# Early mixing of a feed-forward's partial sums, and three inner layer norms as two VectorE instructions per block

## The chip, the core and the metric

The kernel runs on one core of a Trainium2 chip, and its metric is the device time of one execution, in microseconds. Five engines run their own instruction streams and wait for each other through semaphores: TensorE (PE in the rows), VectorE (DVE), ScalarE (ACT), GpSimd (POOL) and SyncE (SP), which issues most of the weight loads.

## What is computed

One encoder layer on x of 512 tokens by 1024 channels, all in float32: four sublayers, each followed by a layer norm over the channels.

```
x = layer_norm(ALPHA * x + 0.5 * swiglu(x, ffn1...), ln1_g, ln1_b)
x = layer_norm(ALPHA * x + hybrid_mixer(x, ...), ln2_g, ln2_b)
x = layer_norm(ALPHA * x + memory_cross_attention(x, mem, ...), ln3_g, ln3_b)
x = layer_norm(ALPHA * x + 0.5 * swiglu(x, ffn2...), ln4_g, ln4_b)
layer_norm(x, g, b) = (x - mean) * rsqrt(var + 1e-5) * g + b
```

The hidden width of each feed-forward is 2816, that is 22 chunks of 128.

## The kernel before

**Split products.** Every matmul operand is split into a high part (ScalarE copies it to a reduced float32 form) and a low part (VectorE subtracts the high part from the original), and each product is three matmuls: lines 829 to 831. Weights come as "units" of 128x1024: SyncE loads a unit into `raw` (three or four slots; a load waits until the unit that was in its slot has been split), ScalarE's `prep` writes `ring_hi`, VectorE's `split` writes `ring_lo`, TensorE uses the pair. `U_MK` + m are the eight units of the memory's key projection, `U_F`, `U_KS`, ... those of the mixer behind it, `U_MV` + k those of the memory's value projection.

**The down projection of a feed-forward** is done in five groups of four hidden chunks ("quads") by a scheme of seven block products in place of eight. `part_high` and `part_low` split its seven left operands, GpSimd's `differences` makes four combinations of the weight blocks (`t_1`, `t_2`, and two in place in `wd`), `products` multiplies, and `add_products` (line 1940) adds each product's two 128x512 tiles out of the accumulators in PSUM onto its place: a quarter of the residual x, or one of four blocks of `partial`. Product q of the last group sits at position q. After the last group the partial blocks are mixed into the four quarters of x: four sums on GpSimd (`mix_products`, lines 682 to 689) and four on VectorE (`mix`, line 1947). The two hidden chunks that are left over (chunks 20 and 21) go through `hidden`, `end_hi`, `end_lo` and `last_down` (first feed-forward) or, by halves of the tokens, through `closing` (second). `last_down` goes over the four accumulator banks 4 to 7 twice; its second pass waits for `add_down` (line 1858) to take the first pass's tiles out.

**A layer norm** goes by four blocks of 128 tokens. VectorE adds the last tiles, takes `bn_stats` and `bn_aggr` (`block_stats`, lines 1864 and 1866); GpSimd makes 1/deviation and a shift with four 128x1 instructions (`inverse_deviation`, lines 705 to 710); ScalarE's `standardize` (line 1420) writes (x - mean) / deviation; VectorE's `gain` (line 1875) multiplies by `ln_g`; GpSimd's `add_bias` (line 717) adds `ln_b` for three of the four blocks and VectorE (line 1882) for the last. Then TensorE turns the block (line 849), and ScalarE and VectorE split the turned block into `xT_hi` and `xT_lo` (`turned_pair`), the operand of what follows.

The first norm runs beside the key projection: `project(U_MK + m)` for m = 0 to 7, with the turn of block b after unit `AFTER_MK[b]`. The second and third run inside `project_tiles` beside the last tiles of the mixer's and the cross attention's output projection; the fourth is the end of `closing`. All orders are written out by hand: an engine does its list in order, and a wait at one instruction holds everything behind it.

Of the kernel before, what the change touches and what calls it, by code (L numbers as in the profile page):

```python
# [29 lines left out]
D = 1024  # L30
# [31 lines left out]
QUADS = 5  # L62
# [27 lines left out]
POOL_BLOCKS = (TB - 1, TB - 1, TB - 1, 2)  # L90
AFTER_MK = (1, 3, 4, 5)
# [27 lines left out]
LAST_PRODUCTS = ((2, 3, 4, 5, 6, 7, 8), (2, 3, 4, 5, 6, 9, 12))  # L119
LAST_GATE = (9, 7)  # L120
# [11 lines left out]
def product_unit(f, d, q):  # L132
    return quad_unit(f, d, (LOOP_PRODUCTS if d < QUADS - 1 else LAST_PRODUCTS[f])[q])

# [89 lines left out]
def program(nc, t, out, x_spill):  # L224
    ctx = ExitStack()
    with ctx:
# [164 lines left out]
        acc_zero, acc_mixed, tiles_mixed = sem("acc_zero"), sem("acc_mixed"), sem("tiles_mixed")  # L391
# [4 lines left out]
        shift_done = sem("shift_done")  # L396
# [111 lines left out]
        def product_of(n):  # L508

            for f in range(2):  # L510
                for d in range(QUADS):
                    for q in range(PRODUCTS):
                        if product_unit(f, d, q) == n:
                            return f, d, q
            return None
# [133 lines left out]
        def _(pool):  # L649
# [13 lines left out]
            def differences(f):  # L663

                with pool.Fori(0, QUADS) as i:
                    made = 4 * QUADS * f
                    b11, b21, b22, b12 = down_part(0), down_part(1), down_part(2), down_part(5)
                    pool.wait_ge(wd_in[0], upto(16 * QUADS * f + 16, i, 16))
                    nc.gpsimd.tensor_tensor(t_1[:, :, :], b12, b11, ALU.subtract).then_inc(t_made, 1)  # L669
                    pool.wait_ge(wd_in[1], upto(16 * QUADS * f + 16, i, 16))  # L670
# [3 lines left out]
                    pool.wait_ge(unit_lo, upto(product_unit(f, 0, 1) + 1, i, LOOP))  # L674
# [3 lines left out]
            def mix_products(f):  # L678

                e, last = partial[f], sums_base(f) + 14 * (QUADS - 1)  # L680
                pool.wait_ge(sums, last + 10)
                nc.gpsimd.tensor_tensor(e[:, 2, :, :], e[:, 2, :, :], e[:, 0, :, :], ALU.add).then_inc(acc_mixed, 1)
                pool.wait_ge(acc_mixed, 4 * f + 1)
                pool.wait_ge(tiles_mixed, 4 * f + 1)
                nc.gpsimd.tensor_tensor(e[:, 0, :, :], e[:, 2, :, :], e[:, 1, :, :], ALU.add).then_inc(acc_mixed, 1)
                pool.wait_ge(sums, last + 12)
                nc.gpsimd.tensor_tensor(e[:, 3, :, :], e[:, 3, :, :], e[:, 2, :, :], ALU.add).then_inc(acc_mixed, 1)
                pool.wait_ge(acc_mixed, 4 * f + 3)
                nc.gpsimd.tensor_tensor(e[:, 1, :, :], e[:, 1, :, :], e[:, 3, :, :], ALU.add).then_inc(acc_mixed, 1)
# [11 lines left out]
            def inverse_deviation(n, b):  # L701
# [4 lines left out]
                nc.gpsimd.tensor_scalar(neg_mean[:, col], mv[:, b, 0:1], -1.0, None, ALU.mult).then_inc(eps_added, 1)  # L706
                pool.wait_ge(eps_added, 2 * count)
                nc.gpsimd.tensor_tensor(rstd[:, col], veps[:, col], expo[:, :], ALU.pow).then_inc(rstd_done, 1)
                pool.wait_ge(rstd_done, count)
# [9 lines left out]
            def layer_norm(n, x, lag):  # L719

                for b in range(TB + lag):
                    if b < TB:
                        inverse_deviation(n, b)
                    if 0 <= b - lag < POOL_BLOCKS[n]:
                        add_bias(n, x, b - lag)
# [36 lines left out]
            mix_products(0)  # L762
# [4 lines left out]
            pool.wait_ge(acc_mixed, 4)  # L767
# [3 lines left out]
            layer_norm(0, xa, 1)  # L771
# [30 lines left out]
            layer_norm(1, xb, 0)  # L802
# [3 lines left out]
            layer_norm(2, xb, 0)  # L806
# [5 lines left out]
            mix_products(1)  # L812
            for b in range(2):
                inverse_deviation(3, b)
            for b in range(2):
                add_bias(3, xb, b)
# [6 lines left out]
        def _(pe):  # L823
# [37 lines left out]
            def ffn(f, n0):  # L861
# [17 lines left out]
                def products(d, qs, i=None):  # L879

                    for q in qs:
# [502 lines left out]
        def _(act):  # L1384
# [55 lines left out]
            def ffn(f, n0):  # L1440
# [17 lines left out]
                def parts_high(d, n, i=None):  # L1458
# [8 lines left out]
                    for q in (4, 5, 6):  # L1467
                        part_high(d, q, i)
# [1029 lines left out]
```

## Time and profile before

| | |
|---|---|
| median of 3 runs | 1266.3 us (1265.57 to 1268.78) |
| the profiled execution | 1265.32 us, its span 1263.5 us |
| TensorE busy | 1225.2 us, 97% of the span |
| VectorE busy | 841.0 us, 67% |
| ScalarE busy | 515.1 us, 41% |
| GpSimd busy | 226.0 us, 18% |
| mean granted clock of TensorE | 0.994 of full speed |

The span goes from the first to the last instruction of the profiled execution; times in the rows count from its start. A busy share is the time in which an engine had an instruction, not how near that is to its peak.

### The profile page before, as it was taken

The page shows a single profiled execution, that of the slowest core. Times are in us where ns is not written, and L with a number is a line of the kernel's source. Part 1 is how long each engine was busy: PE and PEld are TensorE (multiplying, and loading weights), DVE is VectorE, ACT ScalarE, POOL GpSimd, SP SyncE. Part 2 cuts the span into 40 slices and gives each one's busy share as a digit, 9 for nine tenths or more (in the row PEclk, how much of TensorE's full clock was granted, in tenths as well). Part 3 has the DMA queues.
Part 4 walks back from the last instruction along what each step waited for, and adds up shares of the span by engine and source line. Part 5 has one row for each costly group of instructions (what it writes and reads, how often), then busy time and mean ns, then how long its engine had stood idle before and what let it go on. Part 6 is the DMA issues. An engine that isn't in the chain of part 4 may idle for free.

```text
span 1263.5 us, 16261 instructions
## 1 busy us (share of the span) xinstructions
PE 1225.2 (97%) x5995; PEld 1028.0 (81%) x6003; DVE 841.0 (67%) x1120; ACT 515.1 (41%) x800; POOL 226.0 (18%) x178
## 2 busy tenths in 40 slices
PE   8999999999988999999999999999999999999995
PEld 8888888888877788888878878888888888888884
DVE  5484848575986676777764457554858484858487
ACT  5242423233434766476733335442324242424242
POOL 2302020202452100001010030001510202020235
PEclk9999999999998999999999999999999999999998
DMA  9623232333146422212163505213432424242301
GB/s 298 202 71 130 75 125 85 114 92 107 35 149 209 125 69 66 84 51 67 51 217 100 184 20 180 84 51 117 167 101 67 133 66 133 66 133 69 130 1 67
DMA packets 163845, 135.52 MB, mean 107 GB/s; under 512 B 4928, under 2 KB 150352, under 8 KB 162768
## 3 DMA queue, kind: packets, MB, share of 16 engines
q1 hardware_dynamic: 159696, 116.44, 30.4%
q0 software_dynamic: 3888, 18.35, 4.0%
q8 instruction: 35, 0.57, 0.2%
q14 instruction: 18, 0.15, 0.0%
q10 hardware_dynamic: 208, 0.01, 0.0%
HBM read 127.45 MB, written 7.34 MB: 107 GB/s over the span
## 4 chain that ended last, share of the span: by engine, by line
PE 80%; DVE 11%; ACT 3%; POOL 2%; issue 2%; DMA 1%; DVEq 0%; POOLq 0%; ACTq 0%
PE bank L829 17%; PE bank L831 17%; PE bank L830 17%; PE banks_scores L829 8%; PE banks_scores L831 8%; PE banks_scores L830 8%; DVE ring_lo L1827 3%; DVE op_lo L1827 1%; PE bank L1172 1%; DVE xb L1854 1%; PE bank L849 1%; DVE partial L1940 1%; DMA raw<-in_mem_w_k 1%; PE banks_scores L1141 1%; PE bank L1192 1%
## 5 line engine op out<-in xcount | busy, mean ns | idle before, releaser
L829 PE MATMUL bank<-xT_hi,ring_hi 128*128 128x512 f32 (+1 forms) x728 | 279.3, 384 | 2.7 <-DVE ring_lo L1827 2.4
L831 PE MATMUL bank<-xT_hi,ring_lo 128*128 128x512 f32 (+1 forms) x728 | 276.8, 380 | 0.0
L830 PE MATMUL bank<-xT_lo,ring_hi 128*128 128x512 f32 (+1 forms) x728 | 276.6, 380 | 0.0
L1827 DVE TENSOR_TENSOR ring_lo<-raw,ring_hi 128x1024 fp32r<-128x1024 f32 x175 | 232.6, 1337 | 45.9 <-ACT ring_hi L1406 45.2
L1406 ACT ACTIVATE ring_hi<-raw 128x1024 fp32r<-128x1024 f32 x175 | 183.7, 1058 | 162.1 <-PE bank L831 133.4
L829 PEld LDWEIGHTS bank<-xT_hi,ring_hi 128*128 128x128 f32 x728 | 137.0, 188 | 28.0 <-issue 2.4
L831 PEld LDWEIGHTS bank<-xT_hi,ring_lo 128*128 128x128 f32 x728 | 136.9, 188 | 26.5
L830 PEld LDWEIGHTS bank<-xT_lo,ring_hi 128*128 128x128 f32 x728 | 137.0, 188 | 24.6
L829 PE MATMUL banks_scores<-xT_hi,ring_hi 128*128 128x512 f32 (+1 forms) x384 | 142.8, 372 | 0.0
L831 PE MATMUL banks_scores<-xT_hi,ring_lo 128*128 128x512 f32 (+1 forms) x384 | 142.6, 371 | 0.0
L830 PE MATMUL banks_scores<-xT_lo,ring_hi 128*128 128x512 f32 (+1 forms) x384 | 142.6, 371 | 0.0
L830 PEld LDWEIGHTS banks_scores<-xT_lo,ring_hi 128*128 128x128 f32 x384 | 72.3, 188 | 12.6
L831 PEld LDWEIGHTS banks_scores<-xT_hi,ring_lo 128*128 128x128 f32 x384 | 72.3, 188 | 12.5
L829 PEld LDWEIGHTS banks_scores<-xT_hi,ring_hi 128*128 128x128 f32 x384 | 72.3, 188 | 12.4
L830 PE MATMUL bank<-ring_lo,op_hi 128*128 128x512 f32 x200 | 77.8, 389 | 0.0
L829 PE MATMUL bank<-ring_hi,op_hi 128*128 128x512 f32 x200 | 77.8, 389 | 0.0
L831 PE MATMUL bank<-ring_hi,op_lo 128*128 128x512 f32 x200 | 77.8, 389 | 0.0
L1406 ACT ACTIVATE ring_hi<-wd 128x1024 fp32r<-128x1024 f32 x50 | 51.8, 1056 | 56.0 <-PE bank L831 45.0
L676 POOL TENSOR_TENSOR wd<-wd,t 128x1024 f32<-128x1024 f32 x10 | 27.1, 2705 | 246.7 <-DVE ring_lo L1827 246.7
L1896 DVE SCALAR_TENSOR_TENSOR hf<-hf,banks_scores 128x512 f32<-128x512 f32 x21 | 14.4, 688 | 77.4 <-PE banks_scores L831 77.2
L669 POOL TENSOR_TENSOR t<-wd 128x1024 f32<-128x1024 f32 x10 | 24.5, 2450 | 225.5 <-DMA wd<-in_ffn_w_down 225.5
L1827 DVE TENSOR_TENSOR ring_lo<-wd,ring_hi 128x1024 fp32r<-128x1024 f32 x50 | 60.2, 1220 | 1.0 <-ACT ring_hi L1406 1.0
(347 smaller groups left out, 2190.6 us busy)
## 6 DMA issues: line engine op xcount, KB each, us to landing
raw<-in_ffn_w_gate SPq DMA_DIRECT2D x44, 512.0 KB, 3.9
raw<-in_ffn_w_up SPq DMA_DIRECT2D x44, 512.0 KB, 4.0
wd<-in_ffn_w_down SPq DMA_DIRECT2D x20, 1024.0 KB, 5.1
raw<-in_mix_w_in SPq DMA_DIRECT2D x34, 512.0 KB, 3.9
raw<-in_mem_w_k SPq DMA_DIRECT2D x8, 512.0 KB, 4.1
raw<-in_mix_w_out SPq DMA_DIRECT2D x8, 512.0 KB, 3.3
raw<-in_mem_w_v SPq DMA_DIRECT2D x8, 512.0 KB, 3.4
raw<-in_mem_w_q SPq DMA_DIRECT2D x8, 512.0 KB, 5.1
```

The lines of the kernel that those rows point to most:

```text
L669: nc.gpsimd.tensor_tensor(t_1[:, :, :], b12, b11, ALU.subtract).then_inc(t_made, 1)
L676: nc.gpsimd.tensor_tensor(b21, b21, t_2[:, :, :], ALU.subtract).then_inc(t_made, 1)
L829: pe.matmul(dst, hi, mhi, start=start, stop=False)
L830: pe.matmul(dst, hi, mlo, start=False, stop=False)
L831: return pe.matmul(dst, lo, mhi, start=False, stop=stop)
L849: mm = pe.transpose(dst[:, c * P:(c + 1) * P], src[:, (c0 + c) * P:(c0 + c + 1) * P], ident[:, :])
L1141: pe.matmul(dst, q_st[:, H % 2, tok], hh[:, keys], start=False, stop=False)
L1172: mm = pe.transpose(dst[:, col - HALF * b:col - HALF * b + P], prob[:, src:src + P], ident[:, :])
L1192: mm = pe.matmul(bank(7)[:, P * k:end], v, probs_low(*cols), start=False, stop=k == TB - 1, skip_group_check=True)
L1406: nc.scalar.activation(dst, src, copy).then_inc(unit_hi, 1)
L1827: nc.vector.tensor_tensor(dst, src, hi.bitcast(F32), ALU.subtract).then_inc(done, 1)
L1896: nc.vector.scalar_tensor_tensor(out=hf[:, slot_h, :], in0=hf[:, slot_h, :], scalar=0.5, in1=bank(2 * side + 1), op0=ALU.mult, op1=ALU.mul ...
```

## The change

1. In the last quad the products are done in the order 0, 3, 4, 5, 1, 2, 6 (`LAST_ORDER`), so that the four partial blocks are complete after four positions. Their mixing is eight sums on VectorE, three of them between the products' additions; GpSimd's four sums are gone. GpSimd's last weight combination of the last quad waits for the unit at position 4 instead of position 1.
2. In the three inner norms VectorE does two instructions on a block: (x - mean) * g, then times 1/deviation plus b, with the splits of that place between them. ScalarE's `standardize`, GpSimd's `add_bias`, the negated mean and the shift are gone there. The fourth norm keeps all of them for its first two blocks, with the negated mean and shift moved to `last_shift`.
3. Beside the first norm the splits of the units U_MK + 3 to U_MK + 5 sit inside blocks 1 to 3, and the turns follow units 1, 2, 4 and 6 in place of 1, 3, 4 and 5.

```diff
-AFTER_MK = (1, 3, 4, 5)
+AFTER_MK = (1, 2, 4, 6)
+LAST_ORDER = (0, 3, 4, 5, 1, 2, 6)
@@ GpSimd
-                    pool.wait_ge(unit_lo, upto(product_unit(f, 0, 1) + 1, i, LOOP))
+                    pool.wait_ge(unit_lo, upto(product_unit(f, d, 1 if d < QUADS - 1 else 4) + 1, i, LOOP))
-            def mix_products(f):
...
-                nc.gpsimd.tensor_scalar(neg_mean[:, col], mv[:, b, 0:1], -1.0, None, ALU.mult).then_inc(eps_added, 1)
-                pool.wait_ge(rstd_done, count)
-                    if 0 <= b - lag < POOL_BLOCKS[n]:
-                        add_bias(n, x, b - lag)
@@ ScalarE, beside the first norm
-                if m < TB - 1:
-                    standardize(0, xa, m + 1)
-                if m < 2:
-                    prep(U_MK + m + 4)
-                elif m >= 3:
-                    for n in (6, 7) if m == 3 else (m + 4,):
-                        prep(U_MK + n)
+                prep(U_MK + m + 4)
@@ VectorE
+            def normalize(n, x, b, between=()):
...
+                nc.vector.scalar_tensor_tensor(out=x[:, b, :], in0=x[:, b, :], scalar=mv[:, b, 0:1], in1=ln_g[:, :],
+                                               op0=ALU.subtract, op1=ALU.mult).then_inc(gained, 1)
+                for unit in between:
+                    split(unit)
+                dve.wait_ge(rstd_done, count)
+                dve.wait_ge(gained, count)
+                nc.vector.scalar_tensor_tensor(out=x[:, b, :], in0=x[:, b, :], scalar=rstd[:, b:b + 1], in1=ln_b[:, :],
+                                               op0=ALU.mult, op1=ALU.add).then_inc(ln_done, 1)
@@ VectorE, mixing
+                    dst, more, ready_sums, ready_mixed = (
+                        (c11, p1, 2, 0), (p6, p1, 6, 0), (p1, p5, 6, 2), (c12, p1, (12, 10)[f], 3),
+                        (p7, p6, 8, 2), (p5, p7, 8, 5), (c21, p7, (14, 12)[f], 5), (c22, p5, 8, 6))[k]
@@ VectorE, end of the first feed-forward
-                for k in (13, 14):
-                    split(n + k)
+                split(n + 13)
+                mix(3)
+                mix(4)
+                split(n + 14)
+                mix(5)
+                mix(6)
                 hidden(1, n + LAST_GATE[0] + 1, chunk0 + 21)
...
-                mix_second()
-                mix_others(14)
+                mix(7)
...
                     block_stats(0, x, b, sums, last + 14 + 2 * b + 2)
...
+                    normalize(0, x, b, (U_MK + 2 + b,) if b else ())
+                    if b:
+                        turned_pair(T_X1, b - 1)
@@ VectorE, closing
                     low(end_lo[:, 0, :], hf[:, 0, :], end_hi[:, 0, :], end_lo_done)
+                    mix(3)
                     hidden_half(0)
-                    mix_second()
+                    mix(4)
...
                     split(n + 12)
+                    mix(5)
+                    mix(6)
                     hidden_half(1)
-                    mix_others(12)
+                    mix(7)
```

How VectorE's list moves at the end of the first feed-forward, from the last splits to the first tile of `last_down` that is taken out (`xa` is the residual, `partial_80` the partial blocks, `hf` the hidden chunk, `ring_lo` the result of a split). Before:

```order
L1827 TENSOR_TENSOR ring_lo<-raw,ring_hi 128x1024 x3
L1893 TENSOR_TENSOR hf<-sig,banks_scores 128x512
L1896 SCALAR_TENSOR_TENSOR hf<-hf,banks_scores 128x512
L1827 TENSOR_TENSOR end_lo<-hf,end_hi 128x512
L1827 TENSOR_TENSOR ring_lo<-raw,ring_hi 128x1024
L1947 TENSOR_TENSOR xa<-xa,partial_80 128x2x512 x3
L1858 TENSOR_TENSOR xa<-xa,banks_scores 128x512
```

and in the change:

```order
L1815 TENSOR_TENSOR ring_lo<-raw,ring_hi 128x1024 x2
L1956 TENSOR_TENSOR xa<-xa,partial_80 128x2x512
L1956 TENSOR_TENSOR partial_80<-partial_80 128x1024
L1815 TENSOR_TENSOR ring_lo<-raw,ring_hi 128x1024
L1956 TENSOR_TENSOR partial_80<-partial_80 128x1024
L1956 TENSOR_TENSOR xa<-xa,partial_80 128x2x512
L1886 TENSOR_TENSOR hf<-sig,banks_scores 128x512
L1889 SCALAR_TENSOR_TENSOR hf<-hf,banks_scores 128x512
L1815 TENSOR_TENSOR end_lo<-hf,end_hi 128x512
L1815 TENSOR_TENSOR ring_lo<-raw,ring_hi 128x1024
L1956 TENSOR_TENSOR xa<-xa,partial_80 128x2x512
L1846 TENSOR_TENSOR xa<-xa,banks_scores 128x512
```

Four mixing sums now stand ahead of the last hidden chunk, and one in place of three behind it.

VectorE's list beside the key projection, block 2 and the start of block 3. Before:

```order
L1864 BN_STATS stats<-xa 128x6 x2
L1866 BN_AGGR mv<-stats 128x2
L1827 TENSOR_TENSOR ring_lo<-raw,ring_hi 128x1024
L1875 TENSOR_TENSOR xa<-xa,ln_g 128x1024
L1858 TENSOR_TENSOR xa<-xa,bank 128x512 x2
L1864 BN_STATS stats<-xa 128x6 x2
L1866 BN_AGGR mv<-stats 128x2
L1827 TENSOR_TENSOR xT_lo<-banks_scores,xT_hi 128x4x128 x2
L1875 TENSOR_TENSOR xa<-xa,ln_g 128x1024 x2
L1827 TENSOR_TENSOR ring_lo<-raw,ring_hi 128x1024
```

and in the change:

```order
L1852 BN_STATS stats<-xa 128x6 x2
L1854 BN_AGGR mv<-stats 128x2
L1869 SCALAR_TENSOR_TENSOR xa<-xa,mv,ln_g 128x1024
L1815 TENSOR_TENSOR ring_lo<-raw,ring_hi 128x1024
L1875 SCALAR_TENSOR_TENSOR xa<-xa,rstd,ln_b 128x1024
L1815 TENSOR_TENSOR xT_lo<-banks_scores,xT_hi 128x4x128 x2
L1846 TENSOR_TENSOR xa<-xa,bank 128x512 x2
L1852 BN_STATS stats<-xa 128x6 x2
L1854 BN_AGGR mv<-stats 128x2
L1869 SCALAR_TENSOR_TENSOR xa<-xa,mv,ln_g 128x1024
L1815 TENSOR_TENSOR ring_lo<-raw,ring_hi 128x1024
L1875 SCALAR_TENSOR_TENSOR xa<-xa,rstd,ln_b 128x1024
```

A block is finished, with one split inside it, before the next one's tiles are added.

VectorE's list in `closing`, around the second half of the last hidden chunk. Before:

```order
L1827 TENSOR_TENSOR ring_lo<-wd_103,ring_hi 128x1024
L1976 TENSOR_TENSOR hf<-sig,banks_scores 128x256
L1979 SCALAR_TENSOR_TENSOR hf<-hf,banks_scores 128x256
L1827 TENSOR_TENSOR end_lo<-hf,end_hi 128x256
L1947 TENSOR_TENSOR xb<-xb,partial_81 128x2x512 x2
L1875 TENSOR_TENSOR xb<-xb,ln_g 128x1024 x2
```

and in the change:

```order
L1815 TENSOR_TENSOR ring_lo<-wd_103,ring_hi 128x1024
L1956 TENSOR_TENSOR partial_81<-partial_81 128x1024
L1956 TENSOR_TENSOR xb<-xb,partial_81 128x2x512
L1975 TENSOR_TENSOR hf<-sig,banks_scores 128x256
L1978 SCALAR_TENSOR_TENSOR hf<-hf,banks_scores 128x256
L1815 TENSOR_TENSOR end_lo<-hf,end_hi 128x256
L1956 TENSOR_TENSOR xb<-xb,partial_81 128x2x512
L1861 TENSOR_TENSOR xb<-xb,ln_g 128x1024 x2
```

Two sums moved ahead of the hidden half.

## Rows read from the trace of the kernel before

**Rows 1.** The page: the chain that ended last, by engine.

```profile
PE 80%; DVE 11%; ACT 3%; POOL 2%; issue 2%; DMA 1%; DVEq 0%; POOLq 0%; ACTq 0%
```

**Rows 2.** TensorE's timeline: start us, duration, instruction [idle before it, its releaser].

```profile
355.66 0.47 PE L829 MATMUL banks_scores<-ring_hi,end_hi 128*128 128x512 f32 x1 [1.48 <-DVE end_lo L1827]
361.25 0.50 PE L829 MATMUL banks_scores<-ring_hi,end_hi 128*128 128x512 f32 x1 [2.58 <-DVE xa L1858]
385.84 0.58 PE L829 MATMUL bank<-memT_hi,ring_hi 128*128 128x256 f32 x1 [4.97 <-DVE ring_lo L1827]
395.90 1.17 PE L849 MATMUL banks_scores<-ident,xa 128*128 128x128 f32 x8 [1.09 <-DVE xT_lo L1827]
402.66 0.40 PE L829 MATMUL bank<-xT_hi,ring_hi 128*128 128x512 f32 x1
...
907.95 1.06 PE L849 MATMUL bank<-ident,xb 128*128 128x128 f32 x8 [2.47 <-DVE xb L1882]
924.39 0.50 PE L829 MATMUL bank<-xT_hi,ring_hi 128*128 128x512 f32 x1 [0.99 <-DVE ring_lo L1827]
1233.96 0.50 PE L829 MATMUL bank<-ring_hi,end_hi 128*128 128x512 f32 x1 [0.59 <-DVE partial L1940]
```

**Rows 3.** TensorE's waits, two of them in the second norm: us in total, times, longest.

```profile
PE banks_scores L829 <- DVE ring_lo L1827: 1.7, 2, 1.2
```

**Rows 4.** VectorE's timeline at the end of the first feed-forward.

```profile
316.98 3.50 DVE L1827 TENSOR_TENSOR op_lo<-s,op_hi 128x512 fp32r<-128x512 f32 x2
325.87 0.68 DVE L1940 TENSOR_TENSOR partial<-partial,banks_scores 128x512 f32<-128x512 f32 x1
...
339.26 1.29 DVE L1940 TENSOR_TENSOR partial<-partial,bank 128x512 f32<-128x512 f32 x2
343.81 8.92 DVE L1827 TENSOR_TENSOR ring_lo<-raw,ring_hi 128x1024 fp32r<-128x1024 f32 x3
352.66 0.68 DVE L1893 TENSOR_TENSOR hf<-sig,banks_scores 128x512 f32<-128x512 f32 x1
356.91 3.49 DVE L1947 TENSOR_TENSOR xa<-xa,partial 128x1024 f32<-128x1024 f32 x3
```

**Rows 5.** GpSimd's timeline: a mixing sum, and the power of two blocks of the first norm.

```profile
344.92 3.38 POOL L687 TENSOR_TENSOR partial<-partial 128x1024 f32<-128x1024 f32 x1
364.17 0.57 POOL L708 TENSOR_TENSOR rstd<-veps,expo 128x1 f32<-128x1 f32 x1
379.59 1.41 POOL L708 TENSOR_TENSOR rstd<-veps,expo 128x1 f32<-128x1 f32 x1
```

**Rows 6.** VectorE's and ScalarE's timelines beside the key projection.

```profile
375.44 1.28 DVE L1858 TENSOR_TENSOR xa<-xa,bank 128x512 f32<-128x512 f32 x2
378.21 1.23 DVE L1827 TENSOR_TENSOR xT_lo<-banks_scores,xT_hi 128x512 fp32r<-128x512 f32 x2
379.36 1.21 DVE L1875 TENSOR_TENSOR xa<-xa,ln_g 128x1024 f32<-128x1024 f32 x1
...
393.21 1.06 ACT L1406 ACTIVATE ring_hi<-raw 128x1024 fp32r<-128x1024 f32 x1 [8.48 <-DMA raw<-in_mem_w_k]
```

**Rows 7.** Windows: us, then busy PE, PEld, DVE, ACT, POOL, PEclk, DMA share, GB/s.

```profile
356.00:366.00 10.00, 7.42 (x33) 5.74 (x32) 9.76 (x14) 0.00 (x0) 1.23 (x4) 1.00 0.69 220
374.00:381.00 7.00, 6.87 (x59) 6.63 (x56) 6.50 (x10) 3.38 (x5) 6.51 (x8) 1.00 0.29 75
386.00:391.00 5.00, 5.00 (x25) 5.00 (x26) 4.38 (x5) 0.00 (x0) 0.53 (x1) 0.54 0.96 268
```

**Rows 8.** The end: timelines of VectorE and GpSimd in `closing`.

```profile
1227.08 0.43 DVE L1976 TENSOR_TENSOR hf<-sig,banks_scores 128x256 f32<-128x256 f32 x1
1232.08 1.22 DVE L1947 TENSOR_TENSOR xb<-xb,partial 128x1024 f32<-128x1024 f32 x1 [2.36 <-POOL partial L685]
1247.66 6.53 POOL L717 TENSOR_TENSOR xb<-xb,ln_b 128x1024 f32<-128x1024 f32 x2 [4.14 <-DVE xb L1875]
1256.38 1.28 DVE L2003 SCALAR_TENSOR_TENSOR x_mid<-xb,neg_mean,ln_g 128x1024 f32<-128x1024 f32 x1
```

More of the change, by code:

```diff
@@ L511, in product_of @@
                 for d in range(QUADS):
-                    for q in range(PRODUCTS):
-                        if product_unit(f, d, q) == n:
-                            return f, d, q
+                    for p in range(PRODUCTS):
+                        if product_unit(f, d, p) == n:
+                            return f, d, block_of(d, p)
             return None
@@ L673, in differences @@
                     nc.gpsimd.tensor_tensor(b12, b22, b12, ALU.subtract).then_inc(t_made, 1)
-                    pool.wait_ge(unit_lo, upto(product_unit(f, 0, 1) + 1, i, LOOP))
+                    pool.wait_ge(unit_lo, upto(product_unit(f, d, 1 if d < QUADS - 1 else 4) + 1, i, LOOP))
                     pool.wait_ge(t_made, upto(made + 2, i, 4))
                     nc.gpsimd.tensor_tensor(b21, b21, t_2[:, :, :], ALU.subtract).then_inc(t_made, 1)
-            def mix_products(f):
[L680 to L689, printed above, removed]
+                with pool.Fori(0, QUADS - 1) as i:
+                    group(0, i)
+                group(QUADS - 1)
             def clear_acc(f):
@@ L717, in add_bias, with layer_norm @@
                 nc.gpsimd.tensor_tensor(x[:, b, :], x[:, b, :], ln_b[:, :], ALU.add).then_inc(ln_done, 1)
[L719 to L723, printed above, removed]
-                    if 0 <= b - lag < POOL_BLOCKS[n]:
-                        add_bias(n, x, b - lag)
+            def layer_norm(n):
+                for b in range(TB):
+                    inverse_deviation(n, b)
             step(nc.gpsimd.memset(ident[:, :], 0.0))
@@ L801, in _ @@
             memT_again()
-            layer_norm(1, xb, 0)
+            layer_norm(1)
             pool.wait_ge(om_full, KC)
@@ L877, in tile_of, with products @@
                     return mm
-                def products(d, qs, i=None):
-                    for q in qs:
-                        n = product_unit(f, d, q)
+                def products(d, positions, i=None):
+                    for p in positions:
+                        n, q = product_unit(f, d, p), block_of(d, p)
                         ready(n, i)
-                        pe.wait_ge(op_lo_done, upto(PRODUCTS * (QUADS * f + d) + q + 1, i, PRODUCTS))
+                        pe.wait_ge(op_lo_done, upto(PRODUCTS * (QUADS * f + d) + p + 1, i, PRODUCTS))
                         for bb in range(2):
-                            tile = 2 * q + bb
+                            tile = 2 * p + bb
                             evicted = tile - 3 if tile >= 4 else tile - 1 if tile < 2 else tile - 5
@@ L1966, in add_down @@
                             dve.wait_ge(unit_used, n + 1)
-                        dve.wait_ge(tiles_mixed, 4)
+                        dve.wait_ge(mixed, 8)
+                        dve.wait_ge(sums, last + 14)
                         add_tile(x, j, bank(4 + j % 4), sums)
@@ L2155, in _ @@
             ffn(0, U_FFN1, xa)
-            for m in range(1, KC):
-                split(U_MK + m + 4)
-                if m < TB:
-                    turned_pair(T_X1, m)
+            split(U_MK + 6)
+            split(U_MK + 7)
+            turned_pair(T_X1, 3)
+            for k in range(4):
+                split(U_F + k)
             ropes = [0]
@@ L2397, in project_tiles @@
                     block_stats(ln, xb, b, tile_free, 8 * s + 2 * b + 2)
-                    for n in splits[b]:
-                        split(n)
-                    gain(ln, xb, b)
+                    normalize(ln, xb, b, splits[b])
                     if 1 <= b <= 2:
```

165 lines of the change are left out of this document (81 added, 84 removed).

## The prediction

> **What bounds the kernel now.** I read the page first, then TensorE's waits, then its timeline at each wait, then the other engines there. The chain that ended last is TensorE for 80% and VectorE for 11% [rows 1], so time can be gained only where TensorE stands still, or behind its last matmul. In the stretches that the change touches it stands still 1.48 and 2.58 us at the end of the first feed-forward, 4.97 and 1.09 us beside the first norm, 2.47 and 0.99 us at and behind the third norm, 0.59 us in the closing [rows 2], and 1.7 us in the second norm [rows 3]: 15.9 us, the most that waits can give. Each ends on an instruction of VectorE. So the question is whether VectorE, which loses some waits and gets more instructions, is earlier or later at those points.
>
> What VectorE waits for there is mostly GpSimd. Three splits took 8.92 us [rows 4] while GpSimd mixed; a GpSimd sum then took 3.38 us [rows 5]. The two engines take turns. Two consecutive sums of half that width take 1.29 us, three full ones 3.49 us [rows 4]: so in an undisturbed row of instructions one costs 0.6 us at 512 columns and 1.14 us at 1024. Three splits should be 3.5 us; 5.4 were lost to GpSimd.
>
> **End of the first feed-forward.** GpSimd's last weight combination of the quad now waits for the unit at position 4. Today it falls on two low parts, 3.50 us in place of 1.29 [rows 4], so VectorE reaches its first addition 2.2 us earlier, at 323.6 instead of 325.87. It then has 14 additions (8.4 us), nine splits (10.3), one low part (0.6) and seven mixing sums (8.0) ahead of the last hidden chunk: 27.3 us. The combination has to run now while it splits and mixes; from nothing to one combination of some 2.4 us (3.38 less one VectorE turn), I take 1.2. That gives 352.1 against 352.66 [rows 4]: nearly all that GpSimd's mixing cost goes into doing the mixing. The chunk's low part and TensorE's second pass move by the same 0.55 us, to 355.1. Behind it stands one mixing sum in place of three (3.49 us for three [rows 4]). So the first tile is out about 0.55 + 2.3 = 2.9 us earlier, and the wait of 2.58 us shrinks to some 0.5. **Minus 2.9 us.** The bounds are the two waits together, minus 4.1, and nothing, if the combination holds VectorE two more times.
>
> **Beside the first norm.** VectorE takes the first tile at 357.5. From the additions of a block to the end of its mean it needs 2.8 us (375.44 to 378.21 [rows 6]). The new instruction has a per-partition scalar; the nearest row is x_mid, 1.28 us [rows 8], so 1.2 in a row. Between its two there is 1/deviation, by two small GpSimd instructions: alone the power takes 0.57 us, but beside a VectorE instruction with two operands in SBUF it took 1.41 and ended 0.43 us behind it [rows 5, 6]. So each 128x1 instruction sits out one VectorE instruction, and the second new one waits about 0.5 us behind the split. Block 0: 2.8 + 1.2 + 0.8 + 1.2 = 6.0. Blocks 1 and 2, with a split and a turned pair: 2.8 + 1.2 + 1.14 + 0.5 + 1.2 + 1.2 = 8.0. Block 3 up to the end of its split: 5.1. That is 385.0, with 0.4 for a turned block that is not there yet, when U_MK + 5 is split. TensorE is there earlier: it starts the keys at 363.9, a unit is 24 matmuls of 0.116 us (6.87 us for 59 [rows 7]), so five units and three turns end at 381. The wait of 4.97 us does not go; it moves from U_MK + 4 to U_MK + 5, at about 4 us, one unit later. What was gained is that unit and its turn.
>
> Then loads decide. A unit's load starts when the split of the unit three before it is done. Today that of U_MK + 7 starts with the split at 385.8 and lands at 393.2, with ScalarE standing 8.48 us [rows 6]: 7.4 us. Now U_F's load starts at 385.4, lands at about 392.8, and ScalarE's copies of the keys stand behind it; U_KS comes behind 389.6 likewise. I put TensorE's start on the mixer's first unit at 398.0, against 402.66 [rows 2]: 4.7 us earlier in all, **another minus 1.8 us**. Its ends are 396.3 (no load is late) and 402.7 (all is eaten).
>
> The clock: the half-level stretch (granted 0.54 for 5 us, the 1.2 GHz level) follows the idle of 4.97 us; behind the idle of 2.58 us it stayed at 1.00 [rows 2, 7]. I leave it as today, since a slow unit here ends before ScalarE is free. By the Trainium skill ("TensorE: Matmul & The Clock Gate", HAM oscillation) a wait between groups of matmuls throttles the array again each time; by that rule the idle of some 4 us costs its full price, up to 1.9 us, and the sum would be that much smaller. Whether the trace agrees hangs on the length of the idle, and these rows leave 2.6 to 5 us open.
>
> **Second and third norm.** ScalarE's standardizing and GpSimd's bias sums leave the line between a block's mean and its turn, and the split that stood behind them. TensorE's waits there are 1.7 us [rows 3], 2.47 and 0.99 us [rows 2]. VectorE's new list ends block 3 about 4.8 us earlier in the third norm: 1.2 from the split no longer held by a bias sum, the rest from the chain VectorE, GpSimd, ScalarE, VectorE. The 0.99 us come from the four scalings of x taking turns with GpSimd; they start earlier, but so does GpSimd. **Minus 1.7 and minus 3.4 us**, bounds nothing and minus 5.2 together.
>
> **Closing.** Here VectorE only gets work. Three sums more stand before the first hidden half (3.4 us), less 2.2 for the moved combination, plus 1.2 for meeting it: the half that began at 1227.08 begins at 1229.5, its low part is ready near 1231.3, and TensorE, which could use it at 1230.6, waits some 0.7 to 1 us; the 0.59 us wait behind it falls away, since the wait of 2.36 us for GpSimd's sum is filled [rows 2, 8]. Even. Before the second half stand two sums more, 2.3 us, and TensorE has 1.4 us of slack there: plus 0.8. VectorE then starts the last tiles 1.1 us later, and GpSimd's two bias sums (6.53 us, taking turns [rows 8]), behind which stands the 1/deviation of block 2, end later. **Plus 1.6 us**; ends minus 0.6 and plus 3.
>
> **Sum.** -2.9 - 1.8 - 1.7 - 3.4 + 1.6 = -8.2 us from the profiled execution's 1265.3: 1257.1. The median of the runs is 1.0 higher, so **1258.1 us**. The Trainium skill ("VectorE: DVE Perf Modes", the errata table) prices an SBUF-to-SBUF instruction of 1024 columns at (58 + 1024)/0.96 = 1.13 us as an estimate; the rows have 1.21 and 1.28. By the page the eight new instructions beside the keys would be 1.2 us cheaper and the sum 1256.9. The rows decide.
>
> **Rivals.**
> - *Nothing left of the first norm* (0.13): the wait before U_MK + 5 and the late loads eat the first 4.7 us. For it: VectorE is busy 6.50 of 7 us there [rows 7] and splits now stand inside the blocks. Against: one mixing sum in place of three. 1258.1 + 4.7 = 1262.8.
> - *The closing costs nothing and no load is late* (0.20): for it, GpSimd's sums of 3.38 us are gone everywhere. -6.4 - 1.7 - 3.4, with nothing for the end: 1254.8.
> - *VectorE becomes the bound, slower* (0.05): four sums more per feed-forward are 9.1 us, three wide instructions more per norm and four waits of 0.5 us make 5.6 us, three times 16.8; together 26 us. If none of it is covered, less the 15.9 us of waits, it is plus 10, 1276. It decides once VectorE has no idle time left in these stretches; with 9.76 of 10 us busy at 356 to 366 [rows 7] it is near that in one, with three more it would be so.
> - *The waits move, and no more* (0.07): each wait removed comes back at the next handover: 1266, within 0.3%.
>
> The forecast keeps 0.55, by itself 1255.5 to 1261. The range 1253 to 1263 takes in the faster rival and nearly the first one. 0.3%, 3.8 us, is about what a measurement of this kernel can tell from no change. Faster by more than that, under 1262.5: 0.55 + 0.20 + half of the first rival, 0.82. Within it: 0.12. Slower: 0.06.
>
> **What would show it.** Right: no VectorE split over 1.3 us at 340 to 352; second-pass wait under 1 us; one wait of 3 to 5 us before a 128x256 matmul, ended by a split; U_F's first matmul near 398; no wait at the turns of the third norm; in the closing a new wait on the low half of `end_lo`. Wrong: GpSimd's combination holding VectorE for more than 2.5 us, 128x1 instructions of GpSimd that wait for two VectorE instructions each, or TensorE waiting inside the last products.

## The result, and the profile after

The changed kernel is **slower**: 1274.6 us median of 4 runs (1272.1 to 1275.6) against 1266.3 (1265.6 to 1268.8), a ratio of 1.0042, interval 1.0028 to 1.0057. The forecast was 1258.1 us, with a chance of 0.06 for slower. The profiled execution took 1274.3 us with a span of 1272.3, 8.8 more than before.

The page of the changed kernel: first busy time by engine, then the chain that ended last. The chain's shares add up to 71% only, those of [rows 1] to 99%, so the two chains are not compared here.

```profile
PE 1229.8 (97%) x5995; PEld 1032.7 (81%) x6003; DVE 846.5 (67%) x1137; ACT 500.3 (39%) x788; POOL 180.0 (14%) x137
...
PE 62%; DVE 4%; ACT 2%; issue 1%; DMA 1%; POOL 1%; DVEq 0%; POOLq 0%; ACTq 0%
```

The totals hide it. GpSimd lost a fifth of its work (226.0 us busy before), ScalarE 15 us, VectorE got 5 us. What counts is where TensorE stands still. Its waits in the changed stretches, to be held against [rows 2]:

```profile
338.33 0.47 PE L827 MATMUL banks_scores<-ring_hi,op_hi 128*128 128x512 f32 x1 [0.48 <-DVE xa L1940]
...
359.06 0.47 PE L827 MATMUL banks_scores<-ring_hi,end_hi 128*128 128x512 f32 x1 [4.16 <-DVE end_lo L1815]
368.60 0.50 PE L827 MATMUL bank<-ring_hi,end_hi 128*128 128x512 f32 x1 [2.20 <-DVE xa L1846]
394.75 0.58 PE L827 MATMUL bank<-memT_hi,ring_hi 128*128 128x256 f32 x1 [4.14 <-DVE ring_lo L1815]
409.36 0.47 PE L827 MATMUL bank<-xT_hi,ring_hi 128*128 128x512 f32 x1 [2.20 <-issue]
426.70 0.48 PE L847 MATMUL bank<-ident,fe 128*128 128x128 f32 x1 [6.20 <-DVE fe L2185]
...
1239.36 0.47 PE L827 MATMUL banks_scores<-ring_hi,end_hi 128*128 128x512 f32 x1 [1.60 <-issue]
1254.40 0.50 PE L827 MATMUL banks_scores<-ring_hi,end_hi 128*128 128x512 f32 x1 [0.82 <-DVE end_lo L1815]
```

In the second and third norm no wait of 0.3 us is left. The useful reading is to pair the same matmul in both traces and write down by how much it starts later. "Second pass" is here, as in the prediction, the products of the last hidden chunk on the first token half (355.66 before), and "keys" are the units from `U_MK` on:

| TensorE's matmul | before | after | later by |
|---|---|---|---|
| second pass, first | 355.66 | 359.06 | 3.4 |
| keys, first | 366.8 | 372.6 | 5.8 |
| key unit `U_MK + 4`, first | 385.84 | 386.60 | 0.8 |
| turn of the third block | 390.91 | 389.57 | -1.3 |
| mixer's first unit, `U_F` | 402.66 | 409.36 | 6.7 |
| turn of `fe` | 414.03 | 426.70 | 12.7 |
| 2.3 us of work behind it | 416.38 | 431.03 | 14.7 |
| last wait of the second norm | 768.70 | 781.33 | 12.6 |
| first turn of the third norm | 907.95 | 917.33 | 9.4 |
| mixer of the third norm's tokens | 924.39 | 932.59 | 8.2 |
| closing, second pass | 1230.49 | 1239.36 | 8.9 |
| closing, last tiles | 1245.33 | 1254.40 | 9.1 |

At 351 us, before the first long stop, the kernel is 0.7 us late, behind the wait of 0.48 us at 338.33; at 432 us it is 14.9 us late. In between it is not late all the time: the old wait of 4.97 us in front of `U_MK + 4` and the half clock behind it are gone from that place, and at 390 us TensorE is 1.3 us ahead. Then comes the wait of 4.14 us one unit later. Behind 432 us the kernel wins back 2.3 and 4.4 us in the two norms and 1.0 at the start of the closing, and pays 1.9 there.

**The first stop.** VectorE's timeline before the last hidden chunk, which it begins at 356.06:

```profile
327.07 2.45 DVE L1815 TENSOR_TENSOR ring_lo<-wd,ring_hi 128x1024 fp32r<-128x1024 f32 x1
...
343.98 2.34 DVE L1815 TENSOR_TENSOR ring_lo<-raw,ring_hi 128x1024 fp32r<-128x1024 f32 x2
346.25 1.21 DVE L1956 TENSOR_TENSOR xa<-xa,partial 128x1024 f32<-128x1024 f32 x1
347.38 1.21 DVE L1956 TENSOR_TENSOR partial<-partial 128x1024 f32<-128x1024 f32 x1
352.64 1.22 DVE L1815 TENSOR_TENSOR ring_lo<-raw,ring_hi 128x1024 fp32r<-128x1024 f32 x1 [4.05 <-ACT ring_hi L1404]
```

Nothing was mis-sized in VectorE's own work. It stood 4.05 us for a copy of ScalarE's, and ScalarE stood for a load, that of `U_MK + 1`:

```profile
351.55 1.06 ACT L1404 ACTIVATE ring_hi<-raw 128x1024 fp32r<-128x1024 f32 x1 [4.17 <-DMA raw<-in_mem_w_k]
```

The load was issued in time. The view of the tile `raw`, SP's queue alone, in a window that holds this one issue (342.9), with the time to its landing:

```profile
L566 SPq DMA_DIRECT2D raw<-in_mem_w_k x1: 378/378/378, 342.9 to 342.9; - x1
DMA to landing us min/median/max: 8.6/8.6/8.6
```

The same unit's load before:

```profile
L561 SPq DMA_DIRECT2D raw<-in_mem_w_k x1: 379/379/379, 342.7 to 342.7; - x1
DMA to landing us min/median/max: 3.7/3.7/3.7
```

What else moved is on GpSimd's queue, after the change and then before it:

```profile
341.85 0.58 POOL L693 DMA_DIRECT2D memT_hi<-memT_spill  x1 [13.42 <-PE bank L829]
342.43 0.54 POOL L693 DMA_DIRECT2D memT_lo<-memT_spill  x1
```

```profile
348.38 3.27 POOL L689 TENSOR_TENSOR partial<-partial 128x1024 f32<-128x1024 f32 x1
351.60 0.58 POOL L696 DMA_DIRECT2D memT_hi<-memT_spill  x1
352.18 0.54 POOL L696 DMA_DIRECT2D memT_lo<-memT_spill  x1
```

The two loads that bring the turned memory rows back (1 MB each) stood behind GpSimd's four mixing sums. With the sums gone they start 9.8 us earlier, 1.1 and 0.5 us ahead of the key weights' load. Before, too, the load behind them was late (issued at 352.8, it landed after 9.6 us), but nothing waited for that one. This is theory A.

**The second stop**, 368.60, is of another kind (theory B): TensorE's third tile of the second token half goes into an accumulator bank that VectorE's third addition has to empty first.

```profile
362.23 0.68 DVE L1846 TENSOR_TENSOR xa<-xa,bank 128x512 f32<-128x512 f32 x1
362.94 1.29 DVE L1852 BATCH_NORM_STATS2 stats<-xa 128x6 f32<-128x512 f32 x2
364.26 0.21 DVE L1854 BATCH_NORM_AGGREGATE mv<-stats 128x2 f32<-128x12 f32 x1
364.59 1.28 DVE L1869 SCALAR_TENSOR_TENSOR xa<-xa,mv,ln_g 128x1024 f32<-128x1024 f32 x1
366.66 1.28 DVE L1875 SCALAR_TENSOR_TENSOR xa<-xa,rstd,ln_b 128x1024 f32<-128x1024 f32 x1 [0.78 <-POOL rstd L704]
367.86 1.28 DVE L1846 TENSOR_TENSOR xa<-xa,bank 128x512 f32<-128x512 f32 x2
```

Before, the second and third addition had only the statistics between them (361.11 to 363.27); now a whole normalisation, with its wait for GpSimd, stands there as well.

**The later stops** (theory C) hang on loads. ScalarE's waits before its copies of `U_MK + 7`, `U_F`, `U_F + 1` and `U_F + 3`:

```profile
390.74 1.06 ACT L1404 ACTIVATE ring_hi<-raw 128x1024 fp32r<-128x1024 f32 x1 [3.90 <-DMA raw<-in_mem_w_k]
...
397.17 1.06 ACT L1404 ACTIVATE ring_hi<-raw 128x1024 fp32r<-128x1024 f32 x1 [4.14 <-DMA raw<-in_mix_w_in]
...
404.98 1.06 ACT L1404 ACTIVATE ring_hi<-raw 128x1024 fp32r<-128x1024 f32 x1 [4.32 <-DMA raw<-in_mix_w_in]
...
417.08 1.06 ACT L1404 ACTIVATE ring_hi<-raw 128x1024 fp32r<-128x1024 f32 x1 [8.59 <-DMA raw<-in_mix_w_in]
```

A load may start when the split three units back is done, and these splits were late, each inside its block's norm. ScalarE's last turn stood behind the third of these copies, and the `fz` that feeds the turn of `fe` behind the fourth and the one after it.

**The clock.** Windows of the changed kernel, columns as in [rows 7], behind the waits of 4.16, 2.20, 4.14, 2.20 and 6.20 us:

```profile
359.00:364.00 5.00, 4.94 (x15) 3.95 (x16) 4.70 (x6) 0.14 (x1) 0.00 (x0) 0.66 0.36 105
368.60:373.00 4.40, 4.40 (x14) 3.56 (x15) 3.32 (x5) 0.14 (x1) 1.88 (x2) 0.67 0.02 4
...
394.70:400.50 5.80, 5.75 (x27) 5.75 (x28) 4.75 (x5) 1.28 (x2) 2.59 (x5) 0.50 0.82 283
409.30:413.00 3.70, 3.65 (x16) 3.06 (x17) 2.22 (x2) 0.00 (x0) 2.62 (x5) 1.00 0.85 280
426.70:431.50 4.80, 4.80 (x14) 3.94 (x15) 2.47 (x3) 4.05 (x7) 0.00 (x0) 0.50 0.40 109
```

Four of the five ran partly or wholly at the 1.2 GHz level. Before, only one wait was followed by that (385.84). Pairing the matmuls prices the three new stretches: 1.5 us at 359 to 363, 1.7 at 369 to 374, 2.2 at 427 to 432. Of the 14.9 us lost, 5.4 are clock.

### The profile page after: what moved, and what is told of

Its sections match the earlier page's. It is cut to its first block, busy times and chain, and to the rows that moved or that the text cites. A ratio compares the mean times of both kernels' runs of the same rounds, so it can differ in the third digit from the quotient of the medians.

```text
span 1272.3 us, 16227 instructions
## 1 busy us (share of the span) xinstructions
PE 1229.8 (97%) x5995; PEld 1032.7 (81%) x6003; DVE 846.5 (67%) x1137; ACT 500.3 (39%) x788; POOL 180.0 (14%) x137
## 4 chain that ended last, share of the span: by engine, by line
PE 62%; DVE 4%; ACT 2%; issue 1%; DMA 1%; POOL 1%; DVEq 0%; POOLq 0%; ACTq 0%
PE bank L827 14%; PE bank L829 14%; PE bank L828 14%; PE banks_scores L827 5%; PE banks_scores L829 5%; PE banks_scores L828 5%; DMA raw<-in_mix_w_in 1%; PE bank L1170 1%; DVE ring_lo L1815 1%; PE banks_scores L1139 1%; PE bank L1190 1%; POOL xb L719 1%; ACT prob L1646 1%; PE bank L847 0%; PE bank L1189 0%
## 5 line engine op out<-in xcount | busy, mean ns | idle before, releaser
L1815 DVE TENSOR_TENSOR ring_lo<-raw,ring_hi 128x1024 fp32r<-128x1024 f32 x175 | 228.4, 1313 | 54.2 <-ACT ring_hi L1404 53.6
L1442 ACT ACTIVATE sig<-banks_scores 128x512 f32<-128x512 f32 x21 | 12.6, 599 | 117.1 <-PE banks_scores L829 117.1
```

The costliest lines, as they stand in the source:

```text
L1815: nc.vector.tensor_tensor(dst, src, hi.bitcast(F32), ALU.subtract).then_inc(done, 1)
```

## The experiments

"Before" was run again beside each group; its median differed from chip to chip (1270.0 for the first four runs, 1265.1 for the next four, 1270.0 for the last), so ratios are compared, and the changed kernel stands at 1.0042. The mean granted clock of "before" differed likewise (0.989 to 0.992 in the runs of the first and the last group, 0.991 to 0.994 in the second). A ratio compared across groups can therefore be off by up to these 5 us; where that matters, the pairing of the traces is given too.

**Theory A alone.**

```diff
-            memT_again()
             pool.wait_ge(unit_lo, U_MK)
...
+            pool.wait_ge(unit_lo, U_MK + 2)
+            memT_again()
```

> The changed kernel, with GpSimd's two loads of the turned memory rows (memT_hi, memT_lo, 1 MB each) issued where they were before the change in time: after VectorE's split of the second key unit, not 9.8 us earlier beside the loads of the key weights. Theory A (the earlier loads take the DMA engines from the key unit's weights): the load of U_MK+1 lands 4 us earlier, VectorE's wait of 4.05 us at 348.6 is gone, the second pass starts near 355.2 instead of 359.06 and its matmuls keep the full clock (1.5 us more); the wait in front of the tile of the third addition then grows from 2.2 to about 3 us. Time 4 to 5.5 us under the changed kernel's 1274.6, near 1269.5. Rival (VectorE has too much work there, whatever the loads do): the second pass stays within 1 us of 359 and the time within 1.5 us of 1274.6.

Ratio 1.000 (0.9989 to 1.001), 5.3 us better than the changed kernel. The same load, issued at the same time, and TensorE's first stop as it is now:

```profile
L566 SPq DMA_DIRECT2D raw<-in_mem_w_k x1: 379/379/379, 342.7 to 342.7; - x1
DMA to landing us min/median/max: 4.0/4.0/4.0
...
354.70 0.47 PE L828 MATMUL banks_scores<-ring_hi,end_hi 128*128 128x512 f32 x1
...
363.92 0.50 PE L828 MATMUL bank<-ring_hi,end_hi 128*128 128x512 f32 x1 [2.90 <-DVE xa L1847]
```

8.6 us became 4.0, the second pass starts at 354.7 (355.2 expected), and the next wait grew from 2.20 to 2.90 as expected. The rival, too much work on VectorE, is out for this stop.

**Theory B alone.** The additions and statistics of block 1 ahead of `normalize(0, x, 0)`.

```diff
-                    add_down((2 * b, 2 * b + 1), n + LAST_DOWN[0] + 1)
-                    block_stats(0, x, b, sums, last + 14 + 2 * b + 2)
+                    for c in ((0, 1) if b == 0 else () if b == 1 else (b,)):
+                        add_down((2 * c, 2 * c + 1), n + LAST_DOWN[0] + 1)
+                        block_stats(0, x, c, sums, last + 14 + 2 * c + 2)
                     normalize(0, x, b, (U_MK + 2 + b,) if b else ())
```

> The changed kernel, with one order changed on VectorE: the sums and statistics of token block 1 stand ahead of the normalisation of block 0, as before the change, instead of behind its second instruction. Theory B (TensorE's third output tile of the second token half waits for the third addition, which now stands behind a whole normalisation with its wait for GpSimd): the wait of 2.20 us at 368.60 and the half clock behind it (1.5 us) are gone, the first key unit's matmuls start 3.7 us earlier, at about 369.3 instead of 372.6; time 2 to 4 us under 1274.6, the second pass still at 359. Rival (a wait of the key units swallows it, since VectorE has the same work in the same time): the keys start earlier but the mixer's first unit still starts at 409 and the time is within 1 us of 1274.6.

Ratio 1.0001 (0.9991 to 1.0012), 5.2 us better, above the expected 2 to 4 us. The wait of 2.20 us is gone from the trace, the first stop is still there (4.46 us for 4.16), and by the pairing with the changed kernel TensorE is 4.3 us faster from the second pass to the keys, 1.7 of it clock. Behind the keys nothing more comes: the wait for `fe` is shorter (4.58 for 6.20 us), but `U_F` began at half clock, which it had not. The rival, that the keys' waits swallow it, is out.

**A and B.**

> Both edits in the changed kernel: the loads of the turned memory rows late, and the sums of block 1 ahead of block 0's normalisation. Theories A and B together: second pass near 355.2, no wait at the third addition, the keys' first matmul near 364 to 365.5 (367 before the change), time 7 to 9 us under the changed kernel's, near 1266.5; what is left against the kernel before is then the start of the mixer (mixer's first unit and the turn of fe), 6 to 8 us, less the gains at the second and third norm. Rival (the stretch is bound by VectorE's work): under 3 us gained.

Ratio 0.996 (0.9944 to 0.9977): 10.4 us, the sum of the two (10.5) within the intervals. They are separate losses. The keys now start at 365.2. What is left is the third group:

```profile
386.94 0.58 PE L828 MATMUL bank<-memT_hi,ring_hi 128*128 128x256 f32 x1 [4.14 <-DVE ring_lo L1816]
401.58 0.47 PE L828 MATMUL bank<-xT_hi,ring_hi 128*128 128x512 f32 x1 [2.75 <-DVE ring_lo L1816]
417.58 0.66 PE L848 MATMUL bank<-ident,fe 128*128 128x128 f32 x4 [3.24 <-DVE fe L2187]
```

**Theory C: the order beside the keys**, on top of A and B.

```diff
-AFTER_MK = (1, 2, 4, 6)
+AFTER_MK = (1, 2, 4, 5)
...
+                normalize(0, x, 0)
+                normalize(0, x, 1, (U_MK + 3,))
+                split(U_MK + 4)
+                turned_pair(T_X1, 0)
+                add_down((4, 5), n + LAST_DOWN[0] + 1)
+                block_stats(0, x, 2, sums, last + 14 + 6)
+                split(U_MK + 5)
+                normalize(0, x, 2)
+                turned_pair(T_X1, 1)
+                split(U_MK + 6)
+                add_down((6, 7), n + LAST_DOWN[0] + 1)
+                block_stats(0, x, 3, sums, last + 14 + 8)
+                normalize(0, x, 3, (U_MK + 7,))
+                turned_pair(T_X1, 2)
...
```

> The kernel of the run e3_both, with VectorE's splits of the key units moved ahead: units 4 to 7 as soon as ScalarE's copy can be there, between the blocks' sums and norms, instead of one behind each block's first instruction; the last block's turn stands behind the sixth key unit, not the seventh. Theory C (the late splits hold the raw slots, so the next loads start late, and everything at the start of the mixer hangs on that chain): the wait of 4.14 us before the sixth key unit and its half clock (about 2 us) are gone, the mixer's first unit starts 6 to 9 us earlier, at 393 to 396 instead of 401.6, and the time is 5 to 10 us under e3_both's, a ratio of 0.988 to 0.992 to the kernel before. Rival (the loads run into the spill of x, 2 MB at once, and that decides): the wait only moves to the mixer's second to fourth unit or to the turn of fe, and the time falls by less than 2 us, a ratio of 0.994 to 0.996.

Ratio 0.9918 (0.9902 to 0.9935), 5.3 us better than e3_both by the ratios, the low end of what was expected, and 7.4 us by pairing the two traces. The load waits are gone (one of 0.33 us is left on ScalarE), and with them the waits at `U_F` and `fe`. One new wait took the place of three:

```profile
388.78 1.94 PE L848 MATMUL banks_scores<-ident,xa 128*128 128x128 f32 x8 [5.12 <-DVE xT_lo L1816]
```

The fourth block's turn needs the bank of the third's, whose low half now stood behind the fourth norm. My order removed a chain of loads and made a chain of banks; `U_F` starts at 397.4, not at 393 to 396.

**The stores of x**, on top of that: GpSimd issues each of the four when its block is done.

> The kernel of the run e5_key_order, with GpSimd's four stores of x (512 KB each) issued one by one, each when its block's norm is done, instead of all four behind the last block. Rival of theory C (loads of the mixer's weights run into 2 MB of stores): waits of ScalarE for a mixer weight before the turn of fe shrink from 3 to 8 us to under 2, and the turn of fe starts 3 us or more earlier than in e5_key_order; time 2 to 4 us lower. Theory C alone: the stores are not in the way, time within 1 us of e5_key_order.

Medians 1254.0 and 1254.8 us in the same group, the ranges overlap: within 1 us. With the splits early, issuing the 2 MB of stores at once costs under 1 us. Whether they lengthened the late loads of the changed kernel (6.1 to 10.2 us there) was not tried by itself.

**The closing**, on top of e5_key_order.

```diff
-                    mix(3)
                     hidden_half(0)
+                    mix(3)
                     mix(4)
...
-                    split(n + 12)
                     mix(5)
                     mix(6)
+                    split(n + 12)
                     hidden_half(1)
```

> The kernel of the run e5_key_order with two places changed in VectorE's order of the closing: the first half of the last hidden chunk stands ahead of the fourth mixing sum, and the sixth and seventh mixing sum stand ahead of the split of the last down unit, where VectorE is idle 1.7 us, instead of behind it. Theory D (what the mixing sums cost in the closing is their place, not their time): TensorE's waits of 1.60 us and 0.82 us for the low half of the last hidden chunk shrink to about 0.5 and 0, time 1.5 to 2.5 us under e5_key_order. Rival (VectorE is full there, so that another instruction comes late): within 0.7 us of it.

1252.2 us (1251.7 to 1253.5) against 1254.8 (1253.9 to 1255.7): 2.6 us by the medians, 1.7 by the spans of the two profiled executions. The waits of 1.60 and 0.82 us became these:

```profile
1218.15 0.47 PE L828 MATMUL banks_scores<-ring_hi,end_hi 128*128 128x512 f32 x1 [0.47 <-issue]
1230.55 0.50 PE L828 MATMUL banks_scores<-ring_hi,op_hi 128*128 128x512 f32 x1 [0.76 <-DVE ring_lo L1816]
```

The first fell as expected. The second was expected near 0 and moved to the split that now stands behind the two sums; the last tiles start 0.6 us earlier all the same. Theory D holds for the place of the fourth sum.

**Parts alone.** The kernel before, with the three-operand norm in the second and third norm only:

> The kernel before, with the three-operand norm in the second and third layer norm alone; the mixing of the partial sums, the first norm and the closing stay as they were. By the alignment of the two traces the second norm gained 2.0 us and the third 4.4 us in the changed kernel, in places that the late start of the mixer should not touch: 1266.3 - 6.4 = 1260 us. Rival (what was gained there was only given back from the delay before it, since loads had run ahead while TensorE waited): 1264 to 1266 us.

Ratio 0.9939 (0.9921 to 0.9957), 7.7 us faster than before; in the pairing the second norm gives 2.3 us, the third 4.4, as in the changed kernel. So these gains are real and not a give-back. This run also shows something about the closing, where GpSimd still mixes as in the kernel before. VectorE's and GpSimd's rows in this run,

```profile
1219.37 3.42 DVE L1827 TENSOR_TENSOR ring_lo<-raw,ring_hi 128x1024 fp32r<-128x1024 f32 x1
1222.72 2.87 DVE L1827 TENSOR_TENSOR end_lo<-hf,end_hi 128x512 fp32r<-128x512 f32 x1
...
1218.40 3.32 POOL L682 TENSOR_TENSOR partial<-partial 128x1024 f32<-128x1024 f32 x1 [17.75 <-DVE partial L1955]
1221.80 3.25 POOL L685 TENSOR_TENSOR partial<-partial 128x1024 f32<-128x1024 f32 x1
```

and before, where the same low part ran without delay:

```profile
1226.48 0.70 DVE L1827 TENSOR_TENSOR end_lo<-hf,end_hi 128x512 fp32r<-128x512 f32 x1
...
1224.38 5.06 POOL L682 TENSOR_TENSOR partial<-partial 128x1024 f32<-128x1024 f32 x1 [17.76 <-DVE partial L1940]
```

The same instructions stand beside each other. Before, GpSimd paid: its sum took 5.06 us, VectorE's low part 0.70. Here VectorE paid: the sum took 3.32 us and the split beside it 3.42, the next sum 3.25 and the low part beside it 2.87. TensorE then waited 2.77 us in the closing, where before it did not, and ran at half clock behind it (a window of the columns of [rows 7]):

```profile
1227.46 0.47 PE L833 MATMUL banks_scores<-ring_hi,end_hi 128*128 128x512 f32 x1 [2.77 <-issue]
...
1228.00:1230.00 2.00, 2.00 (x6) 1.53 (x6) 1.69 (x3) 0.00 (x0) 0.23 (x1) 0.50 0.00 0
```

The changed kernel with late memory loads and the whole first norm as before:

> The changed kernel with the loads of the turned memory rows late (as e1_memt_late) and the whole first layer norm and its order as in the kernel before, on ScalarE and GpSimd; the early mixing, the second and third norm and the closing stay changed. If the early mixing is worth what was predicted (second pass 0.5 us earlier, the wait of 2.58 us for the first tile gone): 2.5 to 3 us at the keys' start against e4_inner_norms, of which the first norm's waits for a late load take some back, and the closing costs its 1.6 and 0.8 us: ratio 0.991 to 0.994, at or a little under e4_inner_norms' 0.9939. If the load of the sixth key unit decides the mixer's start whatever happens ahead of it: the wait of 4.97 us grows by what was gained, and the ratio is 0.994 to 0.996.

Ratio 0.9922 (0.9906 to 0.9939), at the good side of what was expected; its interval overlaps that of e4_inner_norms, so by time alone the early mixing is not shown. The pairing shows it: against e4_inner_norms the second pass starts 0.8 us earlier and the matmul behind the 2.58 us wait 3.1 us earlier; that wait is 0.33 us. The wait before `U_MK + 4` is still there with 4.63 us (4.95), and not longer: the late load did not eat the gain. Put beside the changed kernel with late loads alone (e1_memt_late, 1.000), the old first norm is about 10 us better by the ratios (12 by pairing) than the new one in the changed kernel's order.

**The version that beats both.** e8_closing_order, with the stores apart, the third block's low half ahead of the fourth block's sums, and the last turn behind the seventh key unit:

> The kernel of the run e8_closing_order, with the stores of x apart as in e6_spill_apart, the low half of the third block's turn ahead of the fourth block's sums and norm instead of behind them, and the fourth block's turn behind the seventh key unit again. In e8_closing_order TensorE waited 5.12 us at the fourth block's turn for that low half (it frees the bank), and ran about 4 us behind it at half clock. If the place of the low half was the cause: that wait goes, the next one, for the fourth block's norm, is 2 to 3 us long; the mixer's first unit starts 3 to 5 us earlier than in e8_closing_order (394), time 3 to 5 us under it, a ratio of 0.986 to 0.988 to the kernel before. If VectorE's work up to the fourth block's norm bounds the stretch instead, the wait only changes its name and the time falls by under 1.5 us, a ratio of 0.9885 to 0.99.

Ratio **0.9841** (0.9827 to 0.9854), 1249.2 us (1248.9 to 1249.3) beside 1270.0: 20.8 us faster than before in its group. In the group in which "before" ran at 1265.1, it would be 15.9; the profiled executions differ by 16.3 (spans of 1263.5 and 1247.2). Against e8_closing_order the gain is 3.0 us by the medians, and `U_F` starts at 394.7 for 397.7: the low end of what was expected. The ratio lies below the expected range because "before" took 5 us longer in this group than in that of e8_closing_order. Three things changed at once here; that the wait of 5.12 us went and one of 2.79 for the fourth norm came, as expected, speaks for the place of the low half, but no run has it alone. TensorE has one wait over 0.4 us left beside the first norm:

```profile
389.45 1.09 PE L852 MATMUL banks_scores<-ident,xa 128*128 128x128 f32 x8 [2.79 <-DVE xa L1880]
```

## Why the prediction was wrong

Three steps failed: at the end of the first feed-forward only the sums that left GpSimd were counted, not the two loads that stood behind them; beside the first norm only the first tile's bank was priced, not the third's; and between `U_F` and the turn of `fe` nothing was priced at all. The clock, left as it was, cost 5.4 us on top of these. VectorE's own work and the two later norms were right.

**End of the first feed-forward (-2.9).** VectorE's first addition was put at 323.6 and came at 323.55; GpSimd's combination cost 1.3 us where 1.2 was taken (2.45 for 1.14); the hidden chunk was put at 352.1 and came at 356.06, which is the 4.05 us wait for ScalarE later. The sum of VectorE's work was right, and e1_memt_late and e7_first_norm_old show the term itself: minus 3.1 in the second (361.25 became 359.53, in an execution whose start was 1.4 us later). What failed is the step "nearly all that GpSimd's mixing cost goes into doing the mixing": it counted the sums that left GpSimd, not the two loads queued behind them. Plus 3.4 and 1.5 of clock instead of minus 0.55. Of the 3.4, 0.7 are older: TensorE waits 0.48 us at 338.33 for an addition of the last quad, small, but one of the prediction's own signs of being wrong ("TensorE waiting inside the last products").

**"Behind it stands one mixing sum in place of three ... the wait of 2.58 us shrinks to some 0.5."** It did; but I asked only what stands ahead of the first tile. The third tile's bank, one step further in the same list, cost 2.20 us and 1.7 of clock, which e2_take_out_first took away.

**Beside the first norm (-1.8).** The wait before `U_MK + 5`, 4 us, is in the trace with 4.14, and "two small GpSimd instructions, each sits out one of VectorE's" is right for the last two blocks (1.31 and 1.40 us; the second new instruction waits 0.46). The step "TensorE's start on the mixer's first unit at 398.0" failed: 409.36. It starts from a key start that came 8.7 us later (372.6 for 363.9); but with the keys at 365.2 in e3_both `U_F` still came at 401.6. It also let the loads decide only for `U_F` and `U_KS`: between `U_F` and the turn of `fe` I priced nothing, and 6.2 us of wait and 2.2 of clock lay there. In e5_key_order these waits are gone, with the order of splits, norms and turns changed together; the late splits are the cause that fits, their share alone was not run.

**Clock: left as today.** Wrong by 5.4 us over three stretches. In every profiled run idles of 4.14 us and more were followed by half clock. Between 2.2 and 3.3 us, from 300 us on, both happened. The full clock stayed behind 2.20 us (409.36), 2.47 and 2.58 (before), 2.90 (e1_memt_late) and 3.24 (e3_both). Half clock followed 2.20 (368.60), 2.38 (e2_take_out_first), 2.75 (e3_both), 2.81 (e1_memt_late), and also 2.77 (e4_inner_norms, 1227.46) and 2.79 (e9_turn_earlier, 389.45), which had no other such stretch within 300 us ahead of them. So in these runs neither the length of an idle nor a slow stretch before it tells which of the two comes. The Trainium skill ("TensorE: Matmul & The Clock Gate", HAM oscillation) describes a kernel whose waits of some 3 to 5 us between groups throttle the array each time; the trace agrees for the waits of 4.14 us and more, and does not for the 3.24 us of e3_both.

**Second and third norm (-1.7, -3.4).** 2.3 and 4.4 measured: right, a little small. **Closing (+1.6).** 1.69 - 0.63 + 0.83 = 1.9 by pairing, and the 0.59 us wait fell away as said: right in size, though the first new wait was 1.60 us where 0.7 to 1 was taken, and a gain of 1.0 ahead of it was not in the sum. The estimate of 1.13 us that I took from the Trainium skill ("VectorE: DVE Perf Modes", the errata table) is under the 1.2 us from start to start that the new instructions take in a row (364.15, 365.36, 366.55 in e5_key_order): the row was the better price.

**The rivals.** *VectorE becomes the bound* had the sign and not the cause: in e9_turn_earlier VectorE does the same instructions and the kernel is 16 to 21 us faster than before. No rival had a transfer that starts earlier.

## What to carry to other kernels

When work leaves an engine, list what stood behind it in that engine's queue, transfers above all: it starts earlier, and its new moment has other traffic. For every instruction inserted between two others ask not only who waits for the next one but who waits for the one after, since a bank or a slot handed back late costs as much as a result. And order two engines' lists by what each handover frees: with the same arithmetic, the order of splits, sums and turns and the moment of two loads were worth 25 us here (1.0042 to 0.9841).

## What the runs showed of the hardware

- The load of one 512 KB unit took 3.7 to 4.0 us to land (before, e1_memt_late), and 8.6 us when 2 MB on another queue had been issued up to 1.1 us ahead of it (the changed kernel).
- From 300 us on, an idle of 2.2 to 3.3 us on TensorE was followed by the full clock in five places of these runs and by half clock in six; two of the six, 2.77 and 2.79 us, stood alone. Behind idles of 4.14 us and more it was always half clock.
- When wide instructions of VectorE and GpSimd run beside each other, either may be the one that is held: GpSimd's sum took 5.06 us with VectorE's low part at 0.70 before, and in e4_inner_norms the sums took 3.3 us with VectorE's split at 3.42 and its low part at 2.87. Why, no run tells.
